# A hybrid decoder layer on one core: the first modulation scale loaded by columns, x transposed raw, the shift added afterwards

## The reference, cut to what matters

```
h   = rmsnorm(x, g_pre_mix) * (1 + sc1) + sh1           # x: 256 prompt rows, 8 sample rows, 1024 wide
sh1, sc1, ... = split(silu(c) @ w_mod + b_mod, 6)       # c: 1 prompt row, 8 sample rows
aq, af, ai, ag, bq, bk, bv, gate_a, gate_b = split(h @ w_in)      # w_in: 1024 x 5632
... recurrence (a) and differential attention (b), for prompt and samples, with a paged key cache ...
x   = x + gt1 * rmsnorm(merged @ w_out, g_post_mix)
x   = x + gt2 * rmsnorm(moe(rmsnorm(x, g_pre_ffn) * (1 + sc2) + sh2), g_post_ffn)
```

## Time and profile before

| | |
|---|---|
| runs | 1260.27, 1262.25, 1268.15 us; median 1262.25 |
| profiled execution | span 1258.5 us; the record gives no other time for it, and the median run is 3.75 us over this span |
| PE busy | 1102.0 us, 88% of the span |
| chain that ended last | DMA 45%, PE 27% of the span; by line w_down 26% and 5%, w_gate_up 13% |
| DMA | 485.30 MB, 386 GB/s on average |

### The profile page before, as it was taken

The page is one execution under the profiler, slowest core; times in us unless marked ns, Lnnn a source line. Parts: engine busy times, 40 slices in busy tenths (PEclk is TensorE's granted clock), DMA queues, the critical chain, the costliest instruction groups (busy, mean ns, idle before and its releaser), DMA issues.

```text
span 1258.5 us, 23992 instructions
## 1 busy us (share of the span) xinstructions
PE 1102.0 (88%) x9856; PEld 456.6 (36%) x9856; DVE 588.2 (47%) x1166; ACT 230.7 (18%) x420; POOL 68.5 (5%) x126
## 2 busy tenths in 40 slices
PE   8999999999988697996887979999966995667996
PEld 4776777785322131321222322333211331112332
DVE  3536744444654252563353544666532552332654
ACT  3002510141311110220111211112100211100212
POOL 0312020250100000000000000000000000000000
PEclk9999999999989897998798999999988998888999
DMA  9979994599899999999999999999999999999995
GB/s 342 312 245 347 317 339 154 187 384 366 284 428 429 426 429 426 429 425 429 426 428 428 428 426 393 409 424 427 428 427 428 427 426 430 424 431 425 428 428 236
DMA packets 67619, 485.30 MB, mean 386 GB/s; under 512 B 6421, under 2 KB 29450, under 8 KB 40762
## 3 DMA queue, kind: packets, MB, share of 16 engines
q1 hardware_dynamic: 59312, 461.07, 88.9%
q0 software_dynamic: 7104, 19.65, 4.9%
q10 hardware_dynamic: 1130, 3.51, 0.8%
HBM read 479.47 MB, written 4.72 MB: 385 GB/s over the span
## 4 chain that ended last, share of the span: by engine, by line
DMA 45%; PE 27%; DVE 1%; issue 0%; DVEq 0%; ACT 0%; ACTq 0%
DMA big<-in_w_down 26%; PE PB L1247 13%; DMA big<-in_w_gate_up 13%; PE PB L1274 7%; DMA hTG<-in_w_down 5%; PE PB L1214 2%; PE PB L1201 2%; PE PB L1206 1%; PE PB L1229 1%; PE PB L1221 1%; PE PB L1240 0%; PE PB L1186 0%; PE PB L1232 0%; DVE big L1623 0%; DVE big L1620 0%
## 5 line engine op out<-in xcount | busy, mean ns | idle before, releaser
L1247 PE MATMUL PB<-big,cst 128*32 128x512 f32 x2768 | 355.0, 657 | 109.2 <-DMA big<-in_w_gate_up 109.2
L2189 DVE TENSOR_TENSOR tok<-PB,cst 32x512 f32<-32x512 f32 x188 | 129.1, 687 | 261.7 <-ACT cst L1554 259.8
L1247 PEld LDWEIGHTS PB<-big,cst 128*32 128x32 f32 x2768 | 89.0, 115 | 345.2 <-issue 181.1
L1274 PE MATMUL PB<-big,cst 128*32 128x512 f32 x1408 | 166.6, 602 | 12.8 <-DMA big<-in_w_down 12.7
L2165 DVE TENSOR_SCALAR mod<-PB 64x256 f32<-64x256 f32 x96 | 41.0, 427 | 209.1 <-PE PB L1247 208.4
L756 PE MATMUL PB<-hTG,big 128*128 128x264 f32 x576 | 136.5, 391 | 0.4 <-DVE hTG L1617 0.4
L756 PEld LDWEIGHTS PB<-hTG,big 128*128 128x128 f32 x576 | 106.9, 190 | 27.3 <-issue 10.8
L1544 ACT ACTIVATE mod<-PB 64x256 f32<-64x256 f32 x96 | 36.1, 376 | 422.3 <-PE PB L1247 421.7
L1274 PEld LDWEIGHTS PB<-big,cst 128*32 128x32 f32 x1408 | 39.2, 110 | 96.8 <-issue 65.8
L1201 PE MATMUL PB<-wide,att 128*32 128x256 f32 x784 | 57.9, 415 | 5.1 <-DVE att L2159 4.9
L1554 ACT ACTIVATE cst<-PB 128x512 f32<-128x512 f32 x48 | 28.7, 597 | 178.2 <-PE PB L1274 178.2
(11 more groups left out here) (378 smaller groups left out, 970.9 us busy)
## 6 DMA issues: line engine op xcount, KB each, us to landing
big<-in_w_gate_up SPq DMA_DIRECT2D x115, 2048.0 KB, 31.0
big<-in_w_down SPq DMA_DIRECT2D x57, 2048.0 KB, 23.9
hTG<-in_w_gate_up SPq DMA_DIRECT2D x13, 2048.0 KB, 37.1
big<-in_w_mod SPq DMA_DIRECT2D x24, 1024.0 KB, 7.5
big<-in_w_in SPq DMA_DIRECT2D x22, 1024.0 KB, 9.2
hTG<-in_w_down SPq DMA_DIRECT2D x6, 2048.0 KB, 24.0
wide<-in_cache_k POOLq DMA_DIRECT2D x16, 256.0 KB, 6.8
big<-in_w_out SPq DMA_DIRECT2D x4, 1024.0 KB, 10.5
```

The costliest lines, as they stand in the source:

```text
L1247: mm = pe.matmul(GU[32 * j:32 * j + 32, :], mo["xT"][:, (2 * u + r) * M:(2 * u + r + 1) * M], groups(w[:, r * 2 * D:(r + 1) * 2 * D])[:, j ...
L1274: mm = pe.matmul(DN[32 * j:32 * j + 32, :], mo["actT"][:, (4 * u + r) * M:(4 * u + r + 1) * M], w[:, r * D + half * 512:r * D + (half + 1) ...
L2189: mm = dve.tensor_tensor(mo["y"][rows, :], DN[rows, :], mo["y_part"][other, :], ALU.add)
```

## The change

The scale's weights are cut by columns: piece i is all 8 slices k of 256 columns, so it completes two slices of the scale on its own. SP issues x first, then sc0, w_in 4 first half, sc1, w_in 4 second half, sc2, sc3, w_in 5 first half, and only then the four pieces of the shift. c and the constants move from SP's queue to ACT's, three small vectors from ACT's to POOL's, and b_mod becomes rows of vrows. x is transposed as it is; the norms are spread over the partitions by three products with a matrix of ones (norms_out) and multiplied in together with A1. The four tiles of unit 4 advance together, two slices of k at a time, as the pieces of the scale come (first_tile). The shift now joins after unit 4 and the first half of unit 5, so its correction covers six tiles (r4, r5, b4). The splitting of the biases and the first two queries take other places on DVE.

```diff
+            def load_scale(i):
+                src = wmod[:, :, D + 256 * i:D + 256 * (i + 1)]
+                sp.dma_start(sc_pieces[i], src).then_inc(S(f"sc{i}_landed"), 16)
+
             sp.dma_start(x[:, 0:2, :], a["x_prompt"][0].rearrange("(c p) d -> p c d", p=P)).then_inc(S("x_loaded"), 16)
...
+                if n < 2:
+                    load_scale(n)
+                if n == 2:
+                    load_scale(2)
+                    load_scale(3)
...
-                if u == ("in", FIRST, 1):
+                if u == ("in", IN_ORDER[1], 0):
                     for i in range(4):
                         sp.dma_start(sh_pieces[:, i, :, :], wmod[:, 2 * i:2 * i + 2, 0:D]).then_inc(S(f"sh{i // 2}_landed"), 16)
...
+            for dst, src in ((vrows[VLB:VLB + 8, :], a["hgrn_lb"].rearrange("a (k p) -> (a k) p", p=P)),
+                             (vrows[VGA:VGA + 4, :], a["g_hgrn"][0]),
+                             (vrows[VGB:VGB + 1, :], a["g_subln"])):
+                pool.dma_start(dst, src).then_inc(S("vrows_loaded"), 16)
...
+            def scale_part(i):
+
+                if i == 0:
+                    pe.wait_ge(S("first_ready"), FIRST_READY["cT"] + 1)
                 else:
-                    pe.wait_ge(S(f"sh{i // 2}_landed"), 32)
-                    w = sh_pieces[:, i, :, :]
+                    pe.wait_ge(S("first_done"), FIRST_DONE["sc_rows"] + i)
+                pe.wait_ge(S(f"sc{i}_landed"), 16)
+                for k in range(KC):
+                    j = k % 4
+                    mm = pe.matmul(PB[4][32 * j:32 * j + 32, 0:256], cT[:, k, :], sc_pieces[i][:, k, :],
+                                   start=(k < 4), stop=(k >= 4))
+                mm.then_inc(S("sc_full"), 1)
+
+            def scale_cols(i):
+
+                bank = begin(f"m{i}")
+                pe.wait_ge(S("first_done"), FIRST_DONE["sc_rows"] + i + 1)
+                for q in range(2):
+                    mm = pe.matmul(bank[:, 9 * q:9 * q + 9], mod[:, 0, (i % 2) * 256 + q * P:(i % 2) * 256 + (q + 1) * P],
+                                   C("onehot_e")[:, 0:9], start=True, stop=True)
+                full(mm)
+
+            def norms_out():
+
+                bank = begin("rsb")
+                pe.wait_ge(S("first_ready"), FIRST_READY["diag"] + 3)
+                for c in range(NCH):
+                    n = rows_of[c]
+                    mm = pe.matmul(bank[:, c * P:c * P + n], all_ones[0:n, :], rs_diag[0:n, c * P:c * P + n],
+                                   start=True, stop=True)
+                full(mm)
+
+            def first_tile(j, i):
+
+                w = unit("in", FIRST, j // 2)
+                for k in (2 * i, 2 * i + 1):
+                    pe.wait_ge(S("hT_ready"), k + 1)
+                    mm = pe.matmul(PB[j][:, 0:T], w[:, k * 256 + (j % 2) * P:k * 256 + (j % 2 + 1) * P], hT[:, k, :],
+                                   start=(k == 0), stop=(k == KC - 1))
+                if i == 3:
+                    mm.then_inc(S("proj_full"), 1)
...
+                        mm = pe.matmul(PB[4][32 * j:32 * j + 32, 0:256], cT[:, 2 * i + k, :],
+                                       sh_pieces[:, i, k, j * 256:(j + 1) * 256],
+                                       start=(i == 0 and k == 0), stop=(i == 3 and k == 1))
+                mm.then_inc(S("sh_used"), 1)
...
+                pe.wait_ge(S("first_ready"), FIRST_READY["r4"] + 2)
+                for j in range(6):
                     mm = pe.matmul(bank[:, 9 * j:9 * j + 9], r4_rows[:, j * P:(j + 1) * P], C("onehot_e")[:, 0:9],
                                    start=True, stop=True)
...
+                        if u == IN_ORDER[1] and j == 1 and k == 4:
+                            shift_part(2)
+                            shift_part(3)
+                        if u == IN_ORDER[1] and j == 2:
                             pe.wait_ge(S("hT_ready"), KC + k + 1)
...
-                pe.wait_ge(S("xn_ready"), 3)
+                pe.wait_ge(S("x_loaded"), 32)
                 for c in range(NCH):
                     n = rows_of[c]
-                    mm = tr(bank[:, c * P:c * P + n], xn[0:n, c, k * P:(k + 1) * P], n)
+                    mm = tr(bank[:, c * P:c * P + n], x[0:n, c, k * P:(k + 1) * P], n)
...
+            idle_products(5)
+            for k in range(KC):
+                x_T(k)
+            idle_products(2)
+            scale_part(0)
+            norms_out()
+            scale_cols(0)
+            idle_products(3)
+            first_tile(0, 0)
+            first_tile(1, 0)
+            scale_part(1)
+            idle_products(2)
+            scale_cols(1)
             idle_products(4)
-            scale_bias()
-            idle_products(7)
-            scale_part(0)
-            scale_part(1)
-            for k in range(4):
-                x_T(k)
-            scale_part(2)
-            for k in range(4, KC):
-                x_T(k)
-            scale_part(3)
-            first_cols("mt0", 1)
-            idle_products(5)
-            in_T(FIRST, [], [(shift_part, 0), (shift_part, 1)], [(shift_part, 2), (shift_part, 3)], [(first_unit_shift,)])
-            in_T(5, [(first_unit_cols,)], [], [], [])
+            first_tile(2, 0)
+            first_tile(3, 0)
+            for i in (1, 2):
+                first_tile(0, i)
+                scale_part(i + 1)
+                first_tile(1, i)
+                scale_cols(i + 1)
+                first_tile(2, i)
+                first_tile(3, i)
+            for j in range(4):
+                first_tile(j, 3)
+            in_T(5, [(shift_part, 0), (shift_part, 1)],
+                 [(shift_cols_out,), (unit_shift, "r4", FIRST, (0, 1)), (unit_shift, "r5", 5, (0,))], [(first_unit_cols,)], [])
...
+            for dst, src in ((vrows[VC + 8:VC + 72, :], a["c_sample"].rearrange("a (k p) -> (a k) p", p=P)),
+                             (vrows[VC:VC + 8, :], a["c_prompt"].rearrange("a (k p) -> (a k) p", p=P)),
+                             (cst[:, 0:P + E], a["consts"][:, 0:P + E]),
+                             (vrows[VG1:VG1 + 8, :], a["g_pre_mix"].rearrange("a (k p) -> (a k) p", p=P)),
                              (vrows[VG2:VG2 + 8, :], a["g_pre_ffn"].rearrange("a (k p) -> (a k) p", p=P)),
-                             (vrows[VLB:VLB + 8, :], a["hgrn_lb"].rearrange("a (k p) -> (a k) p", p=P)),
-                             (vrows[VGA:VGA + 4, :], a["g_hgrn"][0]),
-                             (vrows[VGB:VGB + 1, :], a["g_subln"])):
+                             (vrows[VBM:VBM + 16, :], a["b_mod"][:, 0:2 * D].rearrange("a (k p) -> (a k) p", p=P))):
...
+            for k in range(4, KC):
                 act.wait_ge(S("aux_full"), AUX[f"xt{k}"] + 1)
                 act.wait_ge(S("aux_free"), AUX[f"xt{k}"])
-                do(act.activation(hT[:, k, :], aux(f"xt{k}")[:, 0:T], ACT.Copy))
+                do(act.activation(hT[:, k, :], aux(f"xt{k}")[:, 0:T], ACT.Copy), "first_done")
                 act.nop().then_inc(S("aux_free"), 1)
+            act.wait_ge(S("aux_full"), AUX["rsb"] + 1)
+            do(act.activation(RS, aux("rsb")[:, 0:T], ACT.Copy), "first_done")
+            act.nop().then_inc(S("aux_free"), 1)
+            for i in range(4):
+                act.wait_ge(S("sc_full"), i + 1)
+                if i >= 2:
+                    act.wait_ge(S("aux_full"), AUX[f"m{i - 2}"] + 1)
+                do(act.activation(mod[:, 0, (i % 2) * 256:(i % 2 + 1) * 256], PB[4][:, 0:256], ACT.Copy), "first_done")
...
+            do(dve.scalar_tensor_tensor(x_sq[:, 1, :], x[:, 1, :], 1.0, x[:, 1, :], ALU.mult, ALU.mult,
+                                        accum_out=sv("ssq", 1, 2)), "ssq_zero")
+            for k in range(4):
+                dve.wait_ge(S("aux_full"), AUX[f"xt{k}"] + 1)
+                copy(hT[:, k, :], aux(f"xt{k}")[:, 0:T])
+                dve.nop().then_inc(S("aux_free"), 1)
+            dve.wait_ge(S("first_done"), FIRST_DONE["rms"] + 1)
+            do(dve.reciprocal(sv("rs"), sv("rs")))
+            for c in range(NCH):
+                n = rows_of[c]
+                ts(rs_diag[0:n, c * P:c * P + n], ident[0:n, 0:n], sv("rs", c, c + 1, n), None, ALU.mult, sem="first_ready")
...
+            dve.wait_ge(S("first_done"), FIRST_DONE["RS"] + 1)
+            dve.wait_ge(S("first_done"), FIRST_DONE["xT_copied"] + 4)
+            tt(hT[:, :, TP:T], hT[:, :, TP:T], RS[:, TP:T].unsqueeze(1).to_broadcast([P, KC, NS]), ALU.mult)
+            for i in range(4):
+                b = bank(f"m{i}")
+                for q in range(2):
+                    k = 2 * i + q
+                    ts(A1[:, k, :], b[:, 9 * q:9 * q + 9], VT[:, VBM + KC + k:VBM + KC + k + 1],
+                       VT[:, VG1 + k:VG1 + k + 1], ALU.add, ALU.mult)
+                free()
+                tt(hT[:, 2 * i:2 * i + 2, TP:T], hT[:, 2 * i:2 * i + 2, TP:T], A1[:, 2 * i:2 * i + 2, 1:9], ALU.mult)
+                for k in (2 * i, 2 * i + 1):
```

(15 more changed lines are left out.)

166 lines of the change are left out of this document (64 added, 102 removed).

## The result

| | before | changed |
|---|---|---|
| median of 5 runs, us | 1262.25 (1260.27 to 1268.15) | 1273.42 (1271.86 to 1276.55) |
| profiled span, us | 1258.5 | 1272.7 |
| ratio changed / before | | 1.0097, 95% interval 1.0072 to 1.0122 |

The change costs 11 us in the medians and 14.2 us between the two profiled executions. The three microseconds between these two differences are the scatter of the profiled executions: that of before lies 3.75 us under the median in its span, that of the changed kernel 0.7 (both medians are over device times, some 1.7 us longer than a span). The prediction was 1266, with 1260 to 1271 around it: the kernel is slower, as the forecast had it, but by far more, and the result lies outside the range. It is nearest the rival that had 12% (small loads behind x, 1271), and 2.4 us above it.

What follows compares the result with a forecast made beforehand. DMA bounds the expert part and PE the dense part, so the end moves with PE's start of unit 6. Terms +7.2 - 3.3 + 1.5 - 1.1 = +4.3 us gave 1266 us, range 1260 to 1271 for 8 in 10.

Steps and rivals of the forecast that it cites:

- small loads behind x: Rival, 12%, at vt: small loads wait behind x's stream; with V = 10.9, +8.9 us, 1271, slower than before.
- V, the time of vt: Start of the kernel: vt, waiting for the last small load, 4.41 us before, was forecast at 6.3.
- from V to the first tile: PE's start: transposes, first scale part, norms and columns at the low clock level; first tile at V + 15.2 = 21.5 us.
- first tile to unit 6, slow tiles included: PE's work behind the first tile: 43.6 us against 36.4, +7.2, plus +1.5 for tiles and scale_part(1) running slow.
- unit 6 to the experts' first load: Behind unit 6: earlier queries remove PE's wait at the scores, -1.1 us.
- from there to the end: The expert part: same work in the same order, moving with unit 6, its gaps unchanged.
- the 24 us that the prediction named as the sign of being wrong: Sign at the first tile: expected between 20 and 22.5 us; prediction wrong if before 17.5 or after 24.
- I take V = 6.3, near the first: Choice for vt between bounds 5.8 and 10.9, since the last vector is issued when x's stream is a microsecond old.
- the near bound: Lower bound of V, 5.8 us: a POOL load at 2 us had landed 2.5 us after its issue.
- The queries: DVE's queries 0 and 1 ahead of vbs: query 2 about 8 us earlier, PE's 1.10 us score wait gone, -1.1 us.
- The fast level comes during the transposes: Rival, 30%, PE's clock at the start: slices cost 0.53, first tile at 18.3, no slow tiles; -0.4 us, 1262.
- Unit 6 isn't there: Rival, 8%, at unit 6: its first half loads late, PE waits 2.7 us or up to 5; 1269 to 1271.

Runs made afterwards that it cites:

- the loads alone in the kernel before: The kernel before with only the placement of loads changed: x first on SP, c and the constants on ACT; 1266.27 us.
- the kernel with x held back and three parts undone: Changed kernel with x waiting for the small loads, shift after four tiles, no six idle products around scale_cols(1); 1269.22 us, ratio 1.0058.

## Why the prediction was wrong, point by point

The step that failed first is the time of vt; others missed the same way. The span's 14.2 us by the steps of the prediction (the stretches are those of the windows above; the sum of the forecasts is its +4.3):

| step | forecast | measured | off by |
|---|---|---|---|
| V, the time of vt | +1.9 | 10.50 - 4.41 = +6.1 | 4.2 |
| from V to the first tile | 15.2 - 20.4 = -5.2 | 17.24 - 20.36 = -3.1 | 2.0 |
| first tile to unit 6, slow tiles included | +7.2 + 1.5 = +8.7 | 46.81 - 36.41 = +10.4 | 1.7 |
| unit 6 to the experts' first load | -1.1 | 197.18 - 196.82 = +0.4 | 1.5 |
| from there to the end | 0 | 1000.97 - 1000.50 = +0.5 | 0.5 |

These are the rows of one execution, 1.0 us over its median. The kernel with idle products of ones does the same work, and its profile has vt +5.3, then -3.1, +10.4 and -1.0 (195.79 us from unit 6 to the experts' first load): +11.6 us, near the 11.2 of the medians. By it the forecast was off by 3.4, 2.1, 1.7 and 0.1. So vt remains the largest miss, and the one behind unit 6 is gone. The first tile, at 27.74 or 26.99, is behind the 24 us that the prediction named as the sign of being wrong.

- **The step that failed is "I take V = 6.3, near the first" bound.** It was priced from both sides, 5.8 and 10.9, and the value was chosen at the wrong end. The reason given, that the last vector is issued when x's stream is a microsecond old, is what the runs refute: even the page table, issued at 1.39 us, half a microsecond behind x, took 5.4 us. Both bounds also count from POOL's last issue (3.3 us foreseen, 3.03 measured), while PE waited for ACT's b_mod, issued at 3.87, and began vt 6.6 us after that. The nearest row was the far one: small loads under full queues had taken 7.6 us. The kernel before loaded its small vectors in the only two or three microseconds in which the queues were empty, and the change gave this place to x. x held back gives vt at 5.08 (shown), the loads alone in the kernel before give 11.68, and 5.8 us at the experts' first load (shown). The prediction weighed a rule of the Trainium skill here (DMA: Bandwidth & Descriptors, Queues, rings and completion order): engines go round their queues packet by packet. The trace doesn't bear out what I drew from it, a V at the near bound. Whether the arbitration or the loads' way to memory makes them late, no run here tells.
- **V to the first tile: the mechanism was right, the size was not.** The low level did last to the first tiles. Eight slices took 6.6 us for the 6.0 that an ACT copy's spacing gave; the norms' three products 1.75 for 0.9 and scale_cols 0.99 for 0.5, since I had priced both at the high level; DVE's way to the first slice took 1.7 for 1.3, ACT's copy 1.07 for 1.2. Nor is the level one step up: in the kernel with x held back and three parts undone, the norms took 1.02 us and scale_cols 0.58, at the high level, and after two waits of 1.07 and 1.05 us the first tiles' eight records took 3.86 again, at the low one.
- **First tile to unit 6.** The counts of products were right, the sum was not: the terms written down add up to 45.4 us, not 45.1, so that the forecast by its own rows is +7.5 and not +7.2 (likewise V + 15.2 reaches the 24.77 of before at V = 9.6, not 9.7). That is 0.3 of the 1.7. From start to start, the scale (3.0), the idle products (1.6), r4 and r5 (+0.85) and b4 (+0.45) took what their rows said, the scale's columns 0.2 less, the wait at r4 was 0.91, as priced. The rest is in the tiles: the first eight records took 3.8 us where 1.9 would do, a loss of 1.9 that was priced at 1.5, and the other 120 took 28.2 us where the rate of before gives 27.4. They stand in smaller groups among other products now; that this is the reason was not tried.
- **The queries.** The wait at the scores went, 1.1 us, as forecast. But I didn't ask what is late next: PE waited 0.78 us for cache_v and 0.73 for the load at 138.43, both new. Both vary: in the kernel with idle products of ones, with vt at 9.70, there was no wait for cache_v and 0.3 us for the load, and the stretch took 195.79 us, 1.0 less than before, as forecast (-1.1). In all nine versions of the changed kernel that were tried it took 195.6 to 196.8. Whether a late start makes these loads late was not tried by itself.
- **The rivals.** "Small loads stand behind x" was the case that came, with its price for V (+6.5 at 10.9) nearly exact; it ended at 1271, short of the measured 1273.4, because it left the other terms of the sum as they were. "The fast level comes during the transposes" (30%) didn't. "Unit 6 isn't there" (8%) didn't: its half unit landed 5.0 us after its issue at 65.24, 4 us ahead of use.
- **What I hadn't combined.** The range let V alone go to its bound. Four terms missed in the same direction in the profiled execution, three in the one with ones. Two of them, V and the way to the first tile, concern the same start, with full queues and a slow PE; that one made the other worse was not tried.

Why the change loses, then. Moving 24 products of the scale behind the first tile moves work, it doesn't take it away, and the move brings its own: r5, six products of columns, two more of b4, six idle products, a wait for the shift. Together the stretch behind the first tile grew by 10.4 us. To pay for this the way to the first tile would have had to shrink by as much. It held 2.0 us in which PE idled and 6.3 us of idle products, 8.3 us that were not work; the rest could only move. The products taken out there were worth 5.2 us, and the transposes at the low level, the norms and the columns took 4.0 of it back. How much of the 6.3 us of idle products is cover for waits and how much could go was not tried: no run takes them out of the kernel before. On top of this comes vt, 4.8 to 6.1 us later.

On the clock: in the changed kernel 24 records of transposes from 12.88 us ran at the low level throughout, and the 16 of the scale behind them too. The Trainium skill (TensorE: Matmul & The Clock Gate, Part 4) says that the full clock doesn't engage for the matrix engine's transpose mode; these rows agree, but don't show that it was the transposes. In the kernel before the level rose within transposes, behind 32 records of the scale, so what decides the moment stays open: four profiles of kernels with the same order on PE up to there (one with ones) have it between 12.5 and 17 us, by an estimate from the records that ran partly at either level (16 of the scale in 1.82 and 1.76 us, 12 of the transposes in 2.70 and 2.76).

## What to carry to other kernels

A small load that gates the first work is to be issued before the big streams, whichever queue it is on: here its price was set by what else was in flight, and it must be bounded by rows with full queues, not by rows with empty ones. Holding the big load back until the small ones have landed is no free cure: it brought vt to 5.08, but PE then waited 2.6 us for x. Before making a first result come sooner by moving work behind it, read how long the engine that bounds idles ahead of it, and how much of its busy time is filler that nothing reads: moved work wins nothing by itself, and every added join or correction is to be paid from these two. Take more than one execution of the start, for here vt alone varied by 1.3 us. And when several terms of a sum rest on the same unknown, their bounds belong to one case, not to separate ones.
